# Compression pages of a hybrid decoder step requested by two engines instead of one

## What is computed

```python
def compress(rows, pe, w1, w2):
    L = rows.shape[1]
    n_cmp = (L - CMP_LEN) // CMP_STRIDE + 1
    idx = np.arange(n_cmp)[:, None] * CMP_STRIDE + np.arange(CMP_LEN)[None, :]
    blk = rows[:, idx] + pe[None, None, :, None, :]
    h = jax.nn.gelu(jnp.einsum('bnlgd,lde->bnge', blk, w1))
    return jnp.einsum('bnge,ef->bngf', h, w2)

# in mixers_sample:
past_n = cache_nsa[page_table].reshape(B, past, 4, N_KV_B, HEAD_DIM)
rows = [jnp.concatenate([past_n[:, :, i], new], axis=1) for i, new in enumerate((kc, vc, ks, vs))]
kcmp = compress(rows[0], cmp_pe_k, cmp_w1_k, cmp_w2_k)
vcmp = compress(rows[1], cmp_pe_v, cmp_w1_v, cmp_w2_v)

# in peer_ffn, for each of 128 picks a token:
act = jax.nn.gelu(jnp.einsum('thkd,td->thk', u_tab[experts], xc))
return jnp.einsum('thk,thkd->td', (gate * act).astype(v.dtype), v_tab[experts])
```

## Time and profile before

| what | before |
|---|---|
| median of three runs | 2712.15 us |
| the profiled execution | 2711.16 us, of it 2709.4 us span |
| TensorE matmuls busy | 1890.4 us (70%) |
| VectorE busy | 1249.4 us (46%) |
| GpSimd busy | 789.9 us (29%) |
| ScalarE busy | 333.1 us (12%) |
| DMA, mean rate | 356 GB/s, 963.70 MB |
| granted TensorE clock, mean | 0.77 of 2.4 GHz |

### The profile page before, as it was taken

One profiled execution on the slowest core, in us unless ns is written; L12 is line 12 of the kernel. 1 busy time (PEld: TensorE's weight loads), 2 busy tenths in 40 slices (PEclk: granted clock), 3 DMA queues, 4 the chain that ended last, 5 costly groups with the idle time before them and its releaser, 6 DMA issues.

```text
span 2709.4 us, 28830 instructions
## 1 busy us (share of the span) xinstructions
PE 1890.4 (70%) x9382; PEld 1084.7 (40%) x9382; DVE 1249.4 (46%) x2312; ACT 333.1 (12%) x779; POOL 789.9 (29%) x594
## 2 busy tenths in 40 slices
PE   8999999879979857566676455454545458883335
PEld 5777665434468735344544112211210026540000
DVE  0500112342036865766796444326343454787551
ACT  0000101421021010010020011001010020011011
POOL 0000000000001154333444344225352474346762
PEclk9999999889989978787888766775766655555555
DMA  9789888965326799999989999999999999999997
GB/s 399 298 347 359 346 319 341 387 226 220 118 100 259 242 387 392 377 379 385 400 333 404 395 362 414 406 361 396 408 404 422 421 421 421 421 412 406 422 422 295
DMA packets 213159, 963.70 MB, mean 356 GB/s; under 512 B 23761, under 2 KB 89298, under 8 KB 122258
## 3 DMA queue, kind: packets, MB, share of 16 engines
q0 software_dynamic: 84512, 627.05, 56.9%
q1 hardware_dynamic: 128354, 332.46, 32.7%
q10 hardware_dynamic: 144, 2.36, 0.2%
HBM read 955.28 MB, written 14.88 MB: 358 GB/s over the span
## 4 chain that ended last, share of the span: by engine, by line
PE 38%; DMA 36%; SPq 9%; DVE 8%; issue 5%; POOL 2%; ACT 1%; POOLq 0%; DVEq 0%; ACTq 0%
DMA sb<-in_peer_v,sb 21%; PE bank L908 13%; DMA sb<-in_nsa_t 10%; SPq L550 6%; PE bank L1271 5%; PE bank L1248 4%; PE bank L1217 4%; DMA sb<-in_peer_u,sb 4%; PE bank L1510 3%; SPq L353 3%; POOL sb L2196 2%; DVE sb L2105 2%; PE bank L1012 2%; PE bank L972 2%; DMA sb<-in_a_v 1%
## 5 line engine op out<-in xcount | busy, mean ns | idle before, releaser
L2105 DVE CUSTOM_DVE_ANT_1 sb<-sb 128x2048 f32<-128x2048 f32 x256 | 585.2, 2292 | 536.5 <-DMA sb<-in_peer_u,sb 533.6
L1510 PE MATMUL bank<-sb 128*32 128x512 f32 x2304 | 480.1, 851 | 445.4 <-DMA sb<-in_peer_v,sb 428.5
L2196 POOL DMA_INDIRECT sb<-in_peer_v,sb x288 | 439.8, 1527 | 599.3 <-PE bank L1510 484.2
L2196 POOL DMA_INDIRECT sb<-in_peer_u,sb x288 | 342.0, 1188 | 661.5 <-DVE sb L2105 366.9
L1271 PE MATMUL bank<-sb 128*128 128x256 f32 x1024 | 295.1, 445 | 142.9 <-DMA sb<-in_nsa_t 142.3
L908 PE MATMUL bank<-sb 128*128 128x288 f32 x1408 | 350.7, 409 | 11.7 <-DMA sb<-in_w_in 11.7
L1271 PEld LDWEIGHTS bank<-sb 128*128 128x128 f32 x1024 | 253.3, 310 | 207.9 <-DMA sb<-in_nsa_t 156.3
L1510 PEld LDWEIGHTS bank<-sb 128*32 128x32 f32 x2304 | 64.7, 126 | 677.8 <-DMA sb<-in_peer_v,sb 614.3
L908 PEld LDWEIGHTS bank<-sb 128*128 128x128 f32 x1408 | 266.3, 191 | 95.1 <-issue 12.2
L882 ACT ACTIVATE sb<-sb 128x32 f32<-128x32 f32 x288 | 83.8, 314 | 597.3 <-PE bank L1510 417.6
L1336 PE MATMUL bank<-sb 128*32 128x512 f32 x128 | 74.1, 738 | 98.4 <-DMA sb<-in_nsa_t 98.4
(11 more groups left out here) (344 smaller groups left out, 1501.5 us busy)
## 6 DMA issues: line engine op xcount, KB each, us to landing
sb<-in_a_k SPq DMA_DIRECT2D x128, 512.0 KB, 7.0
sb<-in_a_v SPq DMA_DIRECT2D x128, 512.0 KB, 6.5
sb<-in_nsa_t SPq DMA_DIRECT2D x384, 128.0 KB, 8.7
sb<-in_w_in SPq DMA_DIRECT2D x44, 1024.0 KB, 9.3
sb<-in_w_out SPq DMA_DIRECT2D x32, 1024.0 KB, 8.9
sb<-in_w_query SPq DMA_DIRECT2D x32, 1024.0 KB, 6.6
sb<-in_nsa_v SPq DMA_DIRECT2D x128, 128.0 KB, 13.0
sb<-in_peer_u,sb POOLq DMA_INDIRECT x288, 16.4
```

What stands on the lines that cost most here:

```text
L1510: mm = pe.matmul(bank[g % 2][32 * c:32 * c + 32, :], diag[j % 4], v_ring[j % 4][:, 512 * c:512 * c + 512], start=(s % 32 == 0), stop=(s % ...
L2105: dve.tensor_tensor_reduce(out=u, in0=u, in1=replica(g), scale=1.0, scalar=0.0, op0=ALU.mult, op1=ALU.add, accum_out=act16[:, r % 2, j:j + ...
L2196: pool.indirect_dma_start(rows[j % 4], None, dram[table], bass.IndirectOffsetOnAxis(ap=idx, axis=0)).then_inc(full[j % 4], 16)
```

## The change

From item 2 on, SyncE asks only for the even pages of each compression item (0, 2, 4, 6). ScalarE asks for the odd ones: at the end of `rows_in` for item n it reads four page numbers into registers, one by one, and issues four DMAs for item n + 2 into the buffer that item n has just left, each page on the same semaphore as before. Items 0 and 1 stay whole with SyncE. All other requests stay where they are.

```diff
-            def later_pages(key, first, table):
-                found = [page(sp, first + j) for j in range(8)]
+            def later_pages(key, first, table, chosen=range(8)):
+                found = [page(sp, first + j) for j in chosen]
                 rows, full = later_room(key)
-                for j, pg in enumerate(found):
+                for j, pg in zip(chosen, found):
                     sp.dma_start(rows[:, 256 * j:256 * j + 256], table(pg).rearrange("a p n -> (a p) n")).then_inc(full, 16)
...
-                    later_pages(("cmp", kv, i), 8 * i, lambda pg: dram["nsa_t"][bass.ds(pg, 1), kv])
+                    later_pages(("cmp", kv, i), 8 * i, lambda pg: dram["nsa_t"][bass.ds(pg, 1), kv],
+                                range(8) if kv == 0 and i < 2 else range(0, 8, 2))
...
+            def odd_pages(n):
+                kv, i = n // (2 * NB), n % (2 * NB)
+                rows, full = later_rows[later_items.slot["cmp", kv, i]], later_full[later_items.slot["cmp", kv, i]]
+                if n == 2:
+                    act.wait_ge(pages_in, 16)
+                for j in range(1, 8, 2):
+                    act.dma_start(rows[:, 256 * j:256 * j + 256],
+                                  dram["nsa_t"][bass.ds(page(act, 8 * i + j), 1), kv].rearrange("a p n -> (a p) n")).then_inc(full, 16)
...
             def background(t):
                 if t in CMP_ROWS:
-                    rows_in(*CMP_ROWS[t])
+                    kv, i = CMP_ROWS[t]
+                    rows_in(kv, i)
+                    if 2 * NB * kv + i + 2 < 4 * NB:
+                        odd_pages(2 * NB * kv + i + 2)
                 if t in CMP_EXP:
                     cmp_exp_of(*CMP_EXP[t])
```

## The result

The changed kernel takes 2687.14 us (median of 13 runs, 2678.01 to 2691.04 us) beside 2705.01 us of the kernel before on the same chips (13 runs, 2695.32 to 2721.7 us). The ratio is 0.9923, with a 95% interval of 0.9906 to 0.9939: some 21 us less, 0.8% (the two medians alone differ by 18 us). The time lies in the stated range and inside the 1%, but the gain is twice the 10 us that were forecast.

A forecast was written before the change was run, and what follows sets the result against it. The prediction took the bytes through the DMA engines to bound the kernel from about 984 us: 2711.2 - 10.5 (page holes) + 0.5 (ScalarE) = 2701 us, forecast as a 2702 us median, range 2684 to 2723 us.

The forecast's parts named there:

- What bounds the kernel: From about 984 us the bytes set the end; TensorE's 133.7 us of page waits cost only about 21 us of holes.
- The much faster rival: Compression: pages set the pace, so most of the 133.7 us of waits comes back, some 2600 us; chance 0.06.
- Why a page item is late: Compression: page packets alternate with gather packets, 23.5 us to land; a second queue makes it 13.3 us.
- nothing moves: Rival for the compression pages: they still land after 24 us, the kernel takes 2711 to 2713 us; chance 0.20.
- What the sooner landing is worth: Compression: only the DMA holes of the pages come back, 10.5 us, with bounds 0 and 21 us.
- the prediction's own signs of being wrong: Landings still at 24 us, TensorE waiting tens of us for diagonals, or a stretch shorter by more than 21 us.
- The hole from 1370 to 1410 us: Compression: DMA share 0.77, 9.8 us free, put down to VectorE, busy 38.16 of 40 us, so not counted as gain.
- the three counted ones: Holes at 1110 to 1130, 1150 to 1170 and 1270 to 1290 us: 3.3 + 3.9 + 3.3 = 10.5 us free.
- SyncE: Compression requests: four reads and four requests fewer an item, but nothing gained from asking; its hold-ups should go.
- ScalarE: Compression: four requests with reads add 4.0 us an item; 0.5 us lost in all, bounds 0 and 33 us.
- The 9.8 us from which it would cost: ScalarE's request group, compression: it costs time once longer than 3.9 us cover plus 5.9 us the bytes have on TensorE.

The follow-up runs named there:

- The run with two of eight pages: Against the kernel before: ScalarE asks for pages 3 and 7 of each compression item from item 2 on, SyncE for the other six; 2685.38 us, ratio 0.9929.
- the kernel with one queue from item 8 on: Against the kernel before: items 2 to 7 split by halves, items 8 to 31 wholly asked for by ScalarE; 2703.16 us, ratio 0.9990.

## Why the prediction was right, and where it was off

**What bounds the kernel** was read rightly: the bytes, not TensorE's waits. 129.8 us of waits for pages went away and 21 us of time. The much faster rival, which the chain of waits suggests, is out. The run with two of eight pages says it most plainly: 68.0 or 3.9 us of waits, a stretch of 585 us in both.

**Why a page item is late** was right in mechanism and number. Turns one for one, now 482 : 482 : 482; 4.0 us of requests and 13.3 us of turns make 17.3 us, and 17.3 us is the median landing. Six pages and two gave 21.8 us for a worked-out 21.4. The rival "nothing moves" is out with it, and so is the rule of the Trainium skill behind it ("DMA: Bandwidth & Descriptors", section "Issuing engines are not separate DMA queues"), for this case: that a second issuing engine saves only the issue time does not hold beside a full queue of gathers. In the changed kernel asking took about as long as before (4.1 us to the end of the last request in the median, 4.8 before), and the late items land 9 us and more sooner. The rule of the same page's section "Queues, rings and completion order", turns around the queue rows, is the one that these traces bear out. In one thing they differ from it: it has a turn drain a packet of about 9 to 17 rows (descriptors), and here a turn is one row.

**What the sooner landing is worth** is the step that was off in size: 10.5 us forecast, 26 us in the compression of each trace, about 21 by the ratio. The bounds given for this term, 0 to 21 us, just hold the ratio's figure; the traces' 26 us lie outside, and a stretch shorter by more than 21 us was one of the prediction's own signs of being wrong. What it was to mean, that the share doesn't read as it was read, came true in part: the holes can't give more than some 20 us, and the rest is in how long packets take (last point). The changed kernel lies 3 us inside the lower end of the range. It would have lain further in had the kernel before not come out 7 us lower over 13 runs (2705.01 us) than over the three from which the forecast was built; that the range held is in part luck. Three things were missing.
- The hole from 1370 to 1410 us, 9.8 us, had been put down to VectorE because it was busy for 38 of 40 us. In the same 40 us of work, and from there to the end of the stretch, VectorE's time is the same before and after, and the hole is smaller after:

```profile
1376.00:1416.00 40.00, 30.83 (x140) 20.72 (x140) 38.27 (x60) 12.01 (x19) 16.92 (x12) 0.82 0.77 278
1376.00:1503.00 127.00, 87.37 (x424) 59.02 (x428) 90.24 (x148) 19.51 (x47) 62.81 (x44) 0.84 0.94 366
```

```profile
1348.00:1388.00 40.00, 32.05 (x148) 20.81 (x140) 37.87 (x61) 10.95 (x16) 17.56 (x12) 0.85 0.91 351
1348.00:1474.00 126.00, 90.19 (x420) 58.18 (x412) 89.15 (x148) 19.10 (x45) 49.02 (x44) 0.85 0.99 393
```

  The share of the 40 us is 0.77 before and 0.91 after, so (1.015 - 0.77) x 40 = 9.8 us free before and 4.2 us after; over the whole 127 us it is 9.5 and 3.2 us. Some 4 us stay though no page is late any more, and 5 to 6 us go with the late pages. VectorE was busy in the hole but was not its cause alone.
- The small holes between the three counted ones. In packet time, items 8 to 31 had some 22 us free before and some 2 us after, all holes together, so 20 us came back where 10.5 us had been counted. This takes 1.02 for a full load, which is what the packet records show in stretches without holes; the prediction's 1.015 was a little low, and 1.02 is more than the rounding of its row's 1.01 allows.
- The gathers' packets were slower before. From 984 to 1450 us q0 had 80.6% of the time for 151.84 MB, 2.47 us per MB, and after the change 84.3% for 161.29 MB, 2.44 us per MB. By the packet records the 8 KB packets of the 148 gathers from item 8 on took 322.9 ns on average before, 318.3 ns after, and 322.4 ns in the kernel with one queue from item 8 on. At 8 packets each on every DMA engine that is some 5 us. The usual packet is not slower (the median is 314 ns before and 315 ns after); it is a few long ones that count, 2.8% of them over 340 ns before and 0.6% after. Nearly half of the long ones before lie within 2 us of a hole, where only a tenth of all packets lie. Why they are longer no run here shows.

**SyncE**: nothing gained from asking, as said. Its requests in the compression took up to 1.33 us instead of 2.93, so the hold-up is smaller with four pages an item and not quite gone. **ScalarE**: the four requests with their reads took 4.3 us from the start of the copy instead of the 4.0 worked out behind it (3.9 us measured so), and TensorE waits for diagonals twice, 8.7 us in sum (twice and 13.0 us before the change). The 9.8 us from which it would cost fits: 8.6 us cost nothing measurable from item 8 on, 15 us cost 138 us against 130 worked out. What the prediction missed is that this bound is about the diagonals in a stretch where the DMA engines are full, and does not hold before 956 us. There the first thing to be late is not a diagonal but the odd pages themselves: asked for 5.6 us later, behind the first gather, they land 11.7 us later, and 12 us are lost. In the changed kernel they go out 2 us ahead of the first gather; how much later they could be is not known.

## What to carry to other kernels

A wait on a DMA is worth what it leaves the DMA engines without work, so read their share before the chain of waits; and do not put such a hole down to whichever engine is busy in it until a kernel without the late transfer has been seen. Small urgent loads beside a deep queue of gathers get one packet in each turn, so spreading their packets over a second hardware queue brings the landing down (here from 26 us and more for the late items to 17), and here a quarter of them was enough, as single waits stayed under 6 us. Before moving requests to an engine with time to spare, work out how long the group may be at its tightest place, not at its usual one, and look at what the request itself will stand behind when it goes out later.

## What the runs showed of the hardware

Three queues share the DMA engines by packet, one row a turn, whatever the size: 482 packets each while q0 moved 3.51 MB and the others 0.43 and 0.44 MB. With one page in four on the third queue it was 515 : 512 : 255, where the third queue held only the 256 packets of two pages. A gather's 8 KB packet held a DMA engine for 0.314 us in the median. A page request on ScalarE costs 1.07 us with the read of its number, and no request of ScalarE's in the kernel with all pages on it took longer than 0.585 us, while some of SyncE's in the kernel before took up to 2.93 us; what held those up was not tried.
